# Dealing the gate products of a decoder merge out between the steps of its prompt attention

## The chip, the cores and the metric

One core of a Trainium2 chip runs the whole program in one launch; everything is float32. The metric is the device time of an execution in microseconds. The kernel before takes 2867.99 us (median of 3 runs, 2867.73 to 2868.76).

## The reference, cut to what matters

One decoder layer for two groups of tokens with the same weights: a prompt of 256 tokens and 8 sequences of 8 new tokens with a paged cache of 2048. So T = 320 token columns. The part that the change concerns:

```
u = RMSNorm(x)                                   # 2048 x 320
z = u @ W_in                                     # q, k, v, small gates, and the merge gates g_A, g_B (2 x 2048 columns)
A = FoX(u); B = NSA(u)                           # attention, 8 heads each, prompt and decode
h = x + W_out( sigmoid(g_A) * (A @ U_A) + sigmoid(g_B) * (B @ U_B) )
y = h + HierMoE(RMSNorm(h))
```

g_A and g_B depend on u alone and so may be computed at any time after the norm; A @ U_A and B @ U_B need the finished attention of prompt and decode tokens.

## The kernel before, in words

The order is written out by hand: seven stages, each a block in which every engine runs its own list, with semaphores between them, and all engines meet at the end of a block.

1. `compress_stage` (the first 278 us of the profile): compressed cache keys and values.
2. `project_stage` (to 803 us): the norm gives `ut`, u in 16 tiles of 128 x 320. Each of 44 weight tiles (1 MB, 128 x 2048, from `w_proj`) comes through the ring `wring` of 4 slots and makes 16 matmuls of 128 x 128 weights by 320 columns (L426). At its end SP stores `ut` to memory (L393) and waits for all stores.
3. `prompt_stage` (to 1076 us): first a chain of small steps for the decode tokens (compressed scores L687, their softmax, transposes L693, importance L697, block selection L701, compressed outputs L703, running sums of the forget gates L714 to L719, one round per head). Then 32 units of prompt attention, (fox, cmp, slc, win) for each of 8 heads, in a pipeline over rounds u = 0 to 33. In round u TensorE computes the scores of unit u (L733 to L743), transposes the probabilities of unit u-1 (L753, L757), and multiplies those of unit u-2 with the values (L773 to L784). VectorE does `front(u)` (mask, maximum) and then `back(u-1)` (scaling by the reciprocal sum); ScalarE does the exponential of u, the copy of the transposed probabilities of u-1 and, for fox and win, the copy of the output of u-2 from PSUM. Outputs of fox go to banks 4 and 5 in turn, those of NSA to 6 and 7.
4. `decode_stage` (to 1530 us): 172 MB of cache stream through four buffers, one of which is the memory of `ut`, another most of `wring`. SP reads the page numbers first and then issues the loads. Once the last values are used it prefetches the first four tiles of the merge (L1009).
5. `merge_stage` (to about 2080 us): `ut` is loaded again (L1275). For each of 16 column tiles j three weight tiles arrive: gate A, gate B, and the stacked U. That is 32 + 16 = 48 matmuls of 320 columns (L1301 for the gates, L1305 for the rest); ScalarE takes the sigmoid from PSUM (L1343), VectorE multiplies and adds (L1370 to L1374). Then the product with W_out (L1327, L1331), 512 columns each.
6. `route_stage` and 7. `experts_stage` (to the end): 52 tiles of expert work; each result is copied to one of NY = 10 buffers (L1953), stored by a ScalarE DMA (L1915), and the buffer is waited for before it is used again (L1952).

Of the kernel before, what the change touches and what calls it, by code (L numbers as in the profile page):

```python
# [19 lines left out]
FP32 = mybir.dt.float32  # L20
# [5 lines left out]
P = 128  # L26
DM = 2048
# [308 lines left out]
def project_stage(nc, m, a):  # L336

    with ExitStack() as ctx:
# [11 lines left out]
        x_in, csw_in, u_out = sem("x_in"), sem("csw_in"), sem("u_out")  # L350
# [13 lines left out]
        def _(sp):  # L364
# [216 lines left out]

def prompt_stage(nc, m, a):

    with ExitStack() as ctx:
        def sem(name):
            return ctx.enter_context(nc.semaphore(name))
        low, mid_ = Pieces(m.flat[:, 0:8192]), Pieces(m.utf)
# [12 lines left out]
        arow = mid_(P, P * FH)  # L600
# [15 lines left out]
        pair, sm, pt, st = mid_(P, 2, NSB * NSB), mid_(P, 2, 384), mid_(P, 2, 384), mid_(P, 2, 8)  # L616
# [20 lines left out]
        @block.sync  # L637
        def _(sp):
            sp.dma_start(cc, a["consts"][:, extra0:extra1]).then_inc(c_in, 16)
            sp.dma_start(m.blockof, a["consts"][0:NSB, extra1:extra1 + PAGES * P]).then_inc(m.rows_in, 16)  # L640
            for dst, name in ((m.row_of, "row_of"), (m.row_win, "row_win"), (m.row_new, "row_new"), (m.row_rep, "row_rep")):
                at, n = C_AT[name]
                sp.dma_start(dst, a["consts"][0:dst.shape[0], at:at + n]).then_inc(m.rows_in, 16)

# [8 lines left out]
        def _(pe):  # L653
            def done(ins):
                ins.then_inc(pe_s, 1)
# [25 lines left out]
            for g in range(G):  # L681
                last = nc.tensor.matmul(m.bank[0:NC_P, 6, g * P:(g + 1) * P], hidp[:, 1, g * NC_P:(g + 1) * NC_P],
                                        m.p("w2_v"), start=True, stop=True)
            done(last)

            for j in range(NB * G):
                last = nc.tensor.matmul(m.bank[32 * (j % 4):32 * (j % 4) + 32, 7, (j // 4) * NC_S:(j // 4 + 1) * NC_S],  # L687
                                        qs[:, j * R * NT:(j + 1) * R * NT],
                                        m.kcs[:, j, 0:NC_S], start=True, stop=True)
            done(last)  # L690
            pe.wait_ge(ds, V_PROBS)
            for t in range(4):
                last = nc.tensor.transpose(m.bank[0:NC_S, 0, t * P:(t + 1) * P], pcs[:, t, :], ident)  # L693
            done(last)
            pe.wait_ge(ds, V_PCT)
# [3 lines left out]
            done(last)  # L699
            pe.wait_ge(ds, V_SEL)  # L700
            done(nc.tensor.transpose(m.bank[0:NSB, 2, 0:P], rank, ident))  # L701
            for j in range(NB * G):
                last = nc.tensor.matmul(m.bank[:, 7, j * 32:(j + 1) * 32], m.vcs[0:NC_S, j, :],  # L703
# [5 lines left out]
            for h in range(FH):  # L709
                if h < 2:  # L710
                    pe.wait_ge(ds, V_SELT)
                else:
                    pe.wait_ge(acs, 2 + h - 1)
                done(nc.tensor.transpose(m.bank[:, 3 + h % 2, 0:P], lf_v[:, :, h], ident))  # L714
# [3 lines left out]
                nc.tensor.matmul(m.bank[:, 5 + h % 2, 0:P], m.c("tri"), lft[:, h % 2, :], start=True, stop=False)  # L718
                done(nc.tensor.matmul(m.bank[:, 5 + h % 2, 0:P], psum_pg[:, h:h + 1].broadcast_to([P, P]),  # L719
# [4 lines left out]
            for u in range(NU + 2):  # L724
                if u < NU:
# [18 lines left out]
                    last.then_inc(sc_done, 1)  # L744
                if 1 <= u <= NU:
# [13 lines left out]
                    last.then_inc(ptr_done, 1)  # L759
                if u >= 2:  # L760
# [3 lines left out]
                    if kind == "fox":  # L764
                        if h >= 2:
                            pe.wait_ge(o_kept, 2 * (h - 2) + 1)
                        ob, first, end = m.bank[:, 4 + h % 2, :], True, True
                    else:
                        if kind == "cmp" and h >= 2:
                            pe.wait_ge(o_kept, 2 * (h - 2) + 2)  # L770
                        ob, first, end = m.bank[:, 6 + h % 2, :], kind == "cmp", kind == "win"
# [16 lines left out]
        def _(act):  # L788
# [5 lines left out]
            nc.scalar.activation(pcs, pcs, ACT.Exp, scale=SCALE).then_inc(exp_done, 1)  # L794
            for h in range(FH):
                act.wait_ge(pe_s, E_PAST + 2 * h)
                if h >= 2:
                    act.wait_ge(pe_s, E_PAST + 2 * (h - 2) + 1)
                nc.scalar.activation(lft[:, h % 2, :], m.bank[:, 3 + h % 2, 0:P], ACT.Copy).then_inc(acs, 1)
            for u in range(NU + 2):  # L800
                if u < NU:
# [4 lines left out]
                    for t in range(2):  # L806
# [3 lines left out]
                        last.then_inc(exp_done, 1)  # L810
                if 1 <= u <= NU:
# [8 lines left out]
                if u >= 2:  # L820
                    v = u - 2
                    kind, h = units[v]
                    if kind in ("fox", "win"):
                        act.wait_ge(pv_done, v + 1)
                        dst = m.zt[:, FQ + h, 0:TP] if kind == "fox" else m.onsa[:, h, 0:TP]
                        nc.scalar.activation(dst, m.bank[:, (4 if kind == "fox" else 6) + h % 2, 0:TP], ACT.Copy
                                             ).then_inc(o_kept, 1)

        @block.vector
        def _(dve):  # L830
# [17 lines left out]
            step(nc.vector.tensor_copy(vcp[0:NC_P, :, :], m.bank[0:NC_P, 6, 0:G * P].rearrange("p (g d) -> p g d", g=G)))  # L848

            dve.wait_ge(pe_s, E_CMPS)  # L850
            s7 = m.bank[:, 7, 0:4 * NC_S].rearrange("p (t n) -> p t n", t=4)
# [16 lines left out]
            pa = pair[:, 0, :].rearrange("p (j i) -> p j i", i=NSB)  # L868
            pb = pair[:, 1, :].rearrange("p (j i) -> p j i", i=NSB)
            nc.vector.tensor_tensor(pa, vi, vj, ALU.is_gt)  # L870
            step(nc.vector.tensor_tensor(pb, vi, vj, ALU.is_equal))
            step(nc.vector.tensor_tensor(pair[:, 1, :], pair[:, 1, :], c("before"), ALU.mult))
            step(nc.vector.tensor_tensor(pair[:, 0, :], pair[:, 0, :], pair[:, 1, :], ALU.add))
# [13 lines left out]
            cmo = m.bank[:, 7, :].rearrange("p (b h t) -> p h b t", b=NB, t=NT)  # L887
# [3 lines left out]
            for h in range(FH):  # L891
                dve.wait_ge(pe_s, E_PAST + 2 * h + 1)
                step(nc.vector.tensor_scalar(m.ncum[:, :, :, h], m.bank[:, 5 + h % 2, 0:P].rearrange(
# [56 lines left out]
def decode_stage(nc, m, a):  # L950

    with ExitStack() as ctx:
# [15 lines left out]
        set_used, wk_in, wv_in = sem("set_used"), sem("wk_in"), sem("wv_in")  # L968
        cum_turned, cum_ready, qp_ready = sem("cum_turned"), sem("cum_ready"), sem("qp_ready")
        new_done, win_done, mx_step, nm_ready, exp_done = (  # L970
# [1188 lines left out]
```

## Time and profile before

| | us |
|---|---|
| median of 3 runs | 2867.99 |
| profiled execution | 2867.84 |
| its span, first to last instruction | 2865.2 |
| TensorE matmuls busy | 2239.0 (78%) |
| VectorE busy | 439.8 (15%) |
| ScalarE busy | 242.7 (8%) |
| prompt units (885 to 1076.4 us): TensorE busy | 120.67 of 191.40 |

A share of busy time is a mean over stages with different limits. In the projection and the merge TensorE is busy without a gap, in the decode stage and the experts the DMA engines are, and in the prompt stage neither is. The granted clock of TensorE is one of two levels, 1.0 (2.4 GHz) or 0.5 (1.2 GHz); a number between them is a mean over a stretch. The row of a float32 matmul counts two instructions for each matmul of the program.

### The profile page before, as it was taken

The numbers are of one execution on the slowest core, as the hardware profiler recorded it, in microseconds if no ns is written. First come the engines' busy times: TensorE is split into PE (matmuls) and PEld (weight loads), VectorE is DVE, ScalarE is ACT, GpSimd is POOL, SyncE is SP. The second block draws the span as 40 slices with busy tenths as digits, with TensorE's granted clock in tenths as the row PEclk, the third lists the DMA queues.
The fourth block names the chain that finished last, engine by engine and source line by source line (L and its number), as shares of the span: only waits on it lengthen the run. The fifth ranks groups of instructions, "written<-read, shape, count | busy, mean of one in ns | idle before, by whom it ended". The sixth has DMA issues, their size and how long they took to land. (4 is left out here: it accounts for less than half of the span.)

```text
span 2865.2 us, 33848 instructions
## 1 busy us (share of the span) xinstructions
PE 2239.0 (78%) x13995; PEld 1383.9 (48%) x13995; DVE 439.8 (15%) x1051; ACT 242.7 (8%) x633; POOL 68.4 (2%) x74
## 2 busy tenths in 40 slices
PE   8998499999756666787886999999974666677752
PEld 7887277777544443334444777774332222232220
DVE  0000100015713331111110000000013111111102
ACT  0000100012101220011010000000010000000000
POOL 0000000000000000000000000000001010000000
PEclk9999799999855557988998999999986787878876
DMA  5543533322220008999995333333246998888875
GB/s 184 158 136 105 180 128 117 120 100 103 101 98 0 0 0 338 413 411 409 411 405 244 130 120 117 126 123 117 103 170 266 408 372 342 366 342 366 359 311 204
DMA packets 117221, 609.24 MB, mean 213 GB/s; under 512 B 18940, under 2 KB 19213, under 8 KB 79309
## 3 DMA queue, kind: packets, MB, share of 16 engines
q1 hardware_dynamic: 100446, 556.72, 50.0%
q0 software_dynamic: 9200, 31.89, 3.0%
q10 hardware_dynamic: 7456, 18.88, 1.7%
q8 instruction: 95, 1.56, 0.2%
q14 instruction: 24, 0.20, 0.0%
HBM read 700.33 MB, written 36.98 MB: 257 GB/s over the span
## 5 line engine op out<-in xcount | busy, mean ns | idle before, releaser
L426 PE MATMUL bank<-ut,wring 128*128 128x320 f32 x1408 | 382.3, 433 | 0.0
L426 PEld LDWEIGHTS bank<-ut,wring 128*128 128x128 f32 x1408 | 267.1, 190 | 110.3 <-issue 1.1
L1301 PE MATMUL bank<-ut,wring 128*128 128x320 f32 x1024 | 280.9, 435 | 17.1 <-DMA ut<-u_kept 17.1
L1301 PEld LDWEIGHTS bank<-ut,wring 128*128 128x128 f32 x1024 | 195.9, 191 | 99.2 <-DMA ut<-u_kept 17.2
L1881 PE MATMUL bank<-wdn,par 128*32 128x512 f32 x512 | 94.4, 873 | 100.6 <-issue 99.8
L1852 PE MATMUL bank<-wgu,arena 128*32 128x512 f32 x1024 | 122.5, 618 | 12.3 <-DMA wgu<-in_w_gu 12.3
L1327 PE MATMUL bank<-wring,arena 128*128 128x512 f32 x256 | 118.4, 605 | 3.1 <-DVE arena L1374 1.6
L247 PE MATMUL bank<-arena,wring 128*128 128x256 f32 x512 | 117.4, 393 | 1.5 <-DMA arena<-in_cmp_kv 1.5
L1863 PE MATMUL bank<-stack,arena 128*128 128x32 f32 x416 | 63.2, 299 | 66.1 <-ACT arena L1905 66.1
L561 DVE RECIPROCAL snew<-snew 128x320 f32<-128x320 f32 x30 | 64.5, 2150 | 313.7 <-ACT snew L530 313.7
L247 PE MATMUL bank<-zt,wring 128*128 128x256 f32 x512 | 111.8, 379 | 0.0
L1863 PEld LDWEIGHTS bank<-stack,arena 128*128 128x128 f32 x416 | 57.2, 213 | 111.5 <-ACT arena L1905 81.4
L247 PEld LDWEIGHTS bank<-arena,wring 128*128 128x128 f32 x512 | 101.0, 198 | 16.3 <-DMA arena<-in_cmp_kv 1.6
L247 PEld LDWEIGHTS bank<-zt,wring 128*128 128x128 f32 x512 | 97.0, 190 | 13.0
L1881 PEld LDWEIGHTS bank<-wdn,par 128*32 128x32 f32 x512 | 18.6, 138 | 135.5 <-issue 133.9
L1327 PEld LDWEIGHTS bank<-wring,arena 128*128 128x128 f32 x256 | 46.0, 189 | 74.8 <-issue 70.3
L1852 PEld LDWEIGHTS bank<-wgu,arena 128*32 128x32 f32 x1024 | 35.2, 117 | 94.9 <-issue 80.5
L1032 PE MATMUL bank<-arena,wring 128*32 128x512 f32 x384 | 51.7, 677 | 34.9 <-DMA arena<-in_kv_k 29.3
L1852 PE MATMUL bank<-wgu_x,arena 128*32 128x512 f32 x640 | 78.6, 634 | 0.0
L1219 DVE TENSOR_REDUCE wring<-bank 128x1 f32<-128x512 f32 x32 | 22.1, 691 | 337.1 <-PE bank L1040 337.1
L1831 PE MATMUL bank<-cst,arena 128*128 128x128 f32 x208 | 37.3, 330 | 44.1 <-DMA arena<-u_tok,tok_at 40.7
L1305 PE MATMUL bank<-zt,wring 128*128 128x320 f32 x256 | 71.5, 432 | 0.0
(392 smaller groups left out, 2125.8 us busy)
## 6 DMA issues: line engine op xcount, KB each, us to landing
wgu<-in_w_gu SPq DMA_DIRECT2D x128, 1024.0 KB, 18.1
wring<-in_w_merge SPq DMA_DIRECT2D x64, 1024.0 KB, 4.8
wdn<-in_w_dn SPq DMA_DIRECT2D x32, 2048.0 KB, 27.9
wring<-in_w_proj SPq DMA_DIRECT2D x44, 1024.0 KB, 4.8
arena<-in_kv_k SPq DMA_DIRECT2D x64, 640.0 KB, 10.0
arena<-in_kv_v SPq DMA_DIRECT2D x64, 640.0 KB, 16.4
wring<-in_kv_k SPq DMA_DIRECT2D x32, 640.0 KB, 15.3
ut<-in_kv_k SPq DMA_DIRECT2D x32, 640.0 KB, 16.9
```

The lines of the kernel that those rows point to most:

```text
L247: last = nc.tensor.matmul(out, w1[kv][:, part * CSTR + l, :], rows[s][:, :, kv, :, l, :].rearrange("p q g j -> p g q j"), start=(l == 0), ...
L426: last = nc.tensor.matmul(m.bank[:, 2 + s % 2, 0:T], m.wring[:, s, k * P:(k + 1) * P], m.ut[:, k, :], start=(k == 0), stop=(k == KD - 1))
L561: step(nc.vector.reciprocal(rn[:, q, :], rn[:, q, :]))
L1032: nc.tensor.matmul(m.bank[rows(j), q, :], qp[:, b % 2, 96 * j + 32 * e:96 * j + 32 * e + 32], k[:, :, h * P:(h + 1) * P], start=(e == 0), ...
L1219: nc.vector.tensor_reduce(mx[:, q:q + 1], m.bank[:, q, :], AX.X, ALU.max)
L1301: last = nc.tensor.matmul(m.bank[:, bk + t, 0:T], w, m.ut[:, k, :], start=(k == 0), stop=(k == KD - 1))
L1305: last = nc.tensor.matmul(m.bank[:, bk + 2 + k // FH, 0:T], w, src, start=(k % FH == 0), stop=(k % FH == FH - 1))
L1327: nc.tensor.matmul(m.bank[:, OB[half][2 * b + c], :], mix[:, k, b * P:(b + 1) * P], m.wring[:, s, i * 1024 + c * 512:i * 1024 + (c + 1) * ...
L1831: last = nc.tensor.transpose(m.bank[:, 2 + kg % 2, j * P:(j + 1) * P], e.xg[:, k * P:(k + 1) * P], m.c("ident"))
L1852: last = nc.tensor.matmul(m.bank[q * TW:(q + 1) * TW, i % 2, :], u[:, k, lo:lo + TW], w[:, k, :], start=(k < 4), stop=(k >= KD - 4))
L1863: last = nc.tensor.matmul(m.bank[:, 4 + i % 2, f * TW:(f + 1) * TW], e.part[:, f * P:(f + 1) * P], e.stack[:, :], start=True, stop=True)
L1881: last = nc.tensor.matmul(m.bank[j * TW:(j + 1) * TW, 6 + i % 2, :], e.hid[:, i % 2, f * TW:(f + 1) * TW], w[:, f, cols:cols + 512], start ...
```

## The change

**The gate products move from the merge to the prompt stage.** The 32 gate tiles (A and B of each j in turn) become 512 matmuls, numbered 0 to 511. A function `fill(upto)` on TensorE issues them up to a given number, and it is called at fixed places of the prompt stage: 8 before the transposes of the compressed probabilities, 4 before the importance, 18 before the selection, 8 in each of the eight rounds of the running sums (94 in all), and the other 418 in three portions of 4 or 5 in each of the 34 rounds: before the scores, before the transposes and before the values. At the first matmul of a tile TensorE waits for the tile's weights and, from the third tile on, for the copy of the tile two before it out of PSUM. The products go to banks 6 and 7 in turn, so the attention's outputs keep one bank each (4 for fox, 5 for NSA), and their first matmul waits for the copy of the head before.

**Their results go to memory.** ScalarE copies each tile to one of two buffers `raw` (a function `keep`, called after the exponential of a round), and SP stores it to a tensor `gates`. SP loads the weights through three slots of `wring`; a load waits for the use of the slot, and each store stands behind a load in SP's list.

**The merge** loads `gates` four column pairs at a time into the memory of `ut`, takes the sigmoid of 640 columns from there, and has 16 matmuls for each j in place of 48. It is written out without loops.

**Around it:** the store of `ut` and its reload go. The table `blockof` is loaded at the start of the decode stage. Several pieces of the prompt stage's working memory move. To save semaphores, the window keys and values of the decode share one, so that the window scores of a sequence wait for its window values too; VectorE's chains in the decode share one; and NY is 8.

```diff
-            sp.wait_ge(z_done, NW)
-            sp.dma_start(a["u_t"], m.ut[:, :, :]).then_inc(u_out, 16)
-            sp.wait_ge(u_out, 16)
...
+EARLY = 94
+FILL = {"probs": 8, "pct": 12, "sel": 30, "past": [30 + 8 * (h + 1) for h in range(FH)],
+        "unit": [EARLY + -(-(2 * KD * KD - EARLY) * (i + 1) // (3 * (4 * H + 2))) for i in range(3 * (4 * H + 2))]}
...
+            sp.wait_ge(pe_s, E_HIDV)
+            for n in range(2 * KD):
+                if n >= 3:
+                    sp.wait_ge(g_done, n - 2)
+                sp.dma_start(m.wring[:, n % 3, :], a["w_gate"][n, :, :]).then_inc(gw_in[n % 3], 16)
+                if n >= 4:
+                    store(n - 4)
+            for n in range(2 * KD - 4, 2 * KD):
+                store(n)
+            for s in range(2):
+                sp.wait_ge(g_out[s], 16 * KD)
...
+            def fill(upto):
+
+                nonlocal given
+                while given < upto:
+                    n, k = given // KD, given % KD
+                    if k == 0:
+                        pe.wait_ge(gw_in[n % 3], 16 * (n // 3 + 1))
+                        if n >= 2:
+                            pe.wait_ge(g_kept, n - 1)
+                    last = nc.tensor.matmul(m.bank[:, 6 + n % 2, 0:T], m.wring[:, n % 3, k * P:(k + 1) * P], m.ut[:, k, :],
+                                            start=(k == 0), stop=(k == KD - 1))
+                    if k == KD - 1:
+                        last.then_inc(g_done, 1)
+                    given += 1
...
+                fill(FILL["past"][h])
...
             for u in range(NU + 2):
+                fill(FILL["unit"][3 * u])
...
+                fill(FILL["unit"][3 * u + 1])
                 if 1 <= u <= NU:
...
+                fill(FILL["unit"][3 * u + 2])
                 if u >= 2:
...
+            def keep(upto):
+
+                nonlocal kept
+                while kept < upto:
+                    act.wait_ge(g_done, kept + 1)
+                    if kept >= 2:
+                        act.wait_ge(g_out[kept % 2], 16 * (kept // 2))
+                    nc.scalar.activation(raw[:, kept % 2, :], m.bank[:, 6 + kept % 2, 0:T], ACT.Copy).then_inc(g_kept, 1)
+                    kept += 1
...
+                keep((FILL["unit"][3 * u - 1] if u else FILL["past"][FH - 1]) // KD)
                 if 1 <= u <= NU:
...
+            keep(2 * KD)
...
-                for t in range(3):
-                    s = (3 * jj + t) % SLOTS
...
+            for j in range(KD):
+                act.wait_ge(g_in[j // GJ % 2], 16 * (j // (2 * GJ) + 1))
+                if j >= 2:
+                    act.wait_ge(mix_ready, j - 1)
+                nc.scalar.activation(sg[:, j % 2, :], gates[:, j // GJ % 2, j % GJ, :], ACT.Sigmoid).then_inc(sig_ready, 1)
...
-NY = 10
+NY = 8
```

TensorE in the prompt stage before, from the first scores (a fox unit) to the scores of the third unit:

```order
L739 MATMUL bank<-zt 128x128
L742 MATMUL bank<-arena,cst 128x128
L739 MATMUL bank<-zt 128x256
L742 MATMUL bank<-arena,cst 128x256
L733 MATMUL bank<-arena,zt 128x15 x2
L757 MATMUL bank<-cst,ut 128x128 x3
L739 MATMUL bank<-zt 128x128
L739 MATMUL bank<-zt 128x256
```

The same place of the changed kernel, where L686 is `fill`:

```order
L686 MATMUL bank<-ut,wring 128x320 x5
L782 MATMUL bank<-zt 128x128
L785 MATMUL bank<-arena,cst 128x128
L782 MATMUL bank<-zt 128x256
L785 MATMUL bank<-arena,cst 128x256
L686 MATMUL bank<-ut,wring 128x320 x12
L776 MATMUL bank<-arena,zt 128x15 x2
L686 MATMUL bank<-ut,wring 128x320 x4
L801 MATMUL bank<-cst,arena 128x128 x3
L686 MATMUL bank<-ut,wring 128x320 x8
L782 MATMUL bank<-zt 128x128
L782 MATMUL bank<-zt 128x256
```

Between scores and transposes there are now four gate matmuls, between the transposes and the next scores eight, four of them before the values and four behind (in the first rounds, which have no values yet, they stand together).

ScalarE in the same rounds of the changed kernel: L865 the exponentials, L849 `keep`, L877 the copy of the transposed probabilities, L885 an output:

```order
L865 ACTIVATE arena<-arena 128x15 x2
L849 ACTIVATE selmask<-bank 128x320
L877 ACTIVATE arena<-bank 128x384
L865 ACTIVATE arena<-arena 128x128
L865 ACTIVATE arena<-arena 128x256
L849 ACTIVATE selmask<-bank 128x320
L877 ACTIVATE arena<-bank 15x256
L885 ACTIVATE zt<-bank 128x256
```

A copy of a gate tile stands behind the exponentials of the round after the one in which the tile's last matmul was issued.

TensorE in the merge before, two column tiles:

```order
L1301 MATMUL bank<-ut,wring 128x320 x32
L1305 MATMUL bank<-zt,wring 128x320 x8
L1305 MATMUL bank<-onsa,wring 128x320 x8
L1301 MATMUL bank<-ut,wring 128x320 x32
L1305 MATMUL bank<-zt,wring 128x320 x8
L1305 MATMUL bank<-onsa,wring 128x320 x8
```

And in the changed kernel, three column tiles:

```order
L1365 MATMUL bank<-zt,wring 128x320 x8
L1365 MATMUL bank<-onsa,wring 128x320 x8
L1365 MATMUL bank<-zt,wring 128x320 x8
L1365 MATMUL bank<-onsa,wring 128x320 x8
L1365 MATMUL bank<-zt,wring 128x320 x8
L1365 MATMUL bank<-onsa,wring 128x320 x8
```

Of each column tile's 48 matmuls the 32 of the gates are gone.

## Rows read from the trace of the kernel before

**Rows 1.** The page, the span in 40 slices of 71.6 us: busy tenths and granted clock.

```profile
PE   8998499999756666787886999999974666677752
PEclk9999799999855557988998999999986787878876
```

**Rows 2.** Windows: length, busy us (x instructions) of PE, PEld, DVE, ACT, POOL; clock, DMA, GB/s.

```profile
700.00:760.00 60.00, 60.00 (x234) 42.58 (x233) 42.76 (x56) 11.54 (x28) 0.00 (x0) 1.00 0.14 51
844.50:885.00 40.50, 24.84 (x123) 20.38 (x123) 17.15 (x39) 4.14 (x11) 0.00 (x0) 0.54 0.00 0
885.00:1076.40 191.40, 120.67 (x377) 81.91 (x376) 63.40 (x265) 49.95 (x176) 0.00 (x0) 0.52 0.00 0
...
1101.50:1124.00 22.50, 17.10 (x272) 6.29 (x268) 4.01 (x10) 0.38 (x1) 0.00 (x0) 1.00 1.02 413
...
1546.00:1551.00 5.00, 4.95 (x9) 3.19 (x10) 0.00 (x0) 0.00 (x0) 0.00 (x0) 0.50 0.92 394
1553.00:1966.00 413.00, 411.38 (x1526) 289.64 (x1525) 22.09 (x48) 13.98 (x32) 0.00 (x0) 1.00 0.34 122
```

**Rows 3.** Timeline of one round in the prompt units: start, duration, [idle before].

```profile
980.77 0.56 DVE L905 TENSOR_TENSOR ut<-bank,arena 128x384 f32<-128x384 f32 x1 [5.89 <-PE bank L742]
...
983.01 0.19 ACT L807 ACTIVATION_READ_ACCUMULATOR ut<-ut 128x1 f32 x1
983.08 0.90 PE L757 MATMUL bank<-cst,ut 128*128 128x128 f32 x3 [2.35 <-DVE ut L935]
```

**Rows 4.** Timeline of the merge's start and two later column tiles.

```profile
1527.13 2.09 SPq L1009 DMA_DIRECT2D wring<-in_w_merge  x4
...
1546.05 20.01 PE L1301 MATMUL bank<-ut,wring 128*128 128x320 f32 x64 [17.09 <-DMA ut<-u_kept]
...
1574.51 17.39 PE L1301 MATMUL bank<-ut,wring 128*128 128x320 f32 x64
...
1600.35 17.39 PE L1301 MATMUL bank<-ut,wring 128*128 128x320 f32 x64
```

**Rows 5.** DMAs: KB each, median us to landing; last, those of tile y_slot.

```profile
wring<-in_w_merge SPq DMA_DIRECT2D x64, 1024.0 KB, 4.8
arena<-in_cmp_kv SPq DMA_DIRECT2D x64, 256.0 KB, 3.0
wring<-in_win_v SPq DMA_DIRECT2D x8, 512.0 KB, 18.0
```

```profile
DMA to landing us min/median/max: 5.8/9.4/10.1
```

**Rows 6.** Waits of SP's queue, 786 to 804 us: total, times, longest.

```profile
SPq L395 <- DMA out_k_nsa<-zt: 6.5, 1, 6.5
SPq L338 <- DMA u_kept<-ut: 6.0, 1, 6.0
```

**Rows 7.** Timeline of the prompt stage's first part, TensorE.

```profile
851.85 1.22 PE L693 MATMUL bank<-cst,arena 128*127 128x128 f32 x4 [4.00 <-DVE arena L857]
...
854.52 1.91 PE L697 MATMUL bank<-arena 127*128 127x33 f32 x8 [1.45 <-DVE arena L861]
...
863.65 0.42 PE L701 MATMUL bank<-cst,arena 128*33 128x128 f32 x1 [7.22 <-DVE arena L875]
...
863.87 6.88 PE L703 MATMUL bank<-arena 127*128 127x32 f32 x32
...
870.55 0.45 PE L714 MATMUL bank<-cst,ut 128*128 128x128 f32 x1
...
872.39 0.42 PE L714 MATMUL bank<-cst,ut 128*128 128x128 f32 x1
```

**Rows 8.** The copies of 320 columns by line L503: min/median/max ns.

```profile
L503 ACT ACTIVATE zt<-bank x30: 437/437/437, 355.8 to 605.5; 128x320 f32 x28, 128x320 f32<-128x320 f32 x2
```

**Rows 9.** Timeline of one decode sequence: issue of window values, window scores.

```profile
1153.16 1.29 SPq L998 DMA_DIRECT2D wring<-in_win_v  x1
...
1173.98 1.06 PE L1068 MATMUL bank<-arena,wring 128*32 128x512 f32 x8
```

More of the change, by code:

```diff
@@ L615, in prompt_stage @@
         selt = piece(P)
-        pair, sm, pt, st = mid_(P, 2, NSB * NSB), mid_(P, 2, 384), mid_(P, 2, 384), mid_(P, 2, 8)
+        pair = [low(P, NSB * NSB), spare(P, NSB * NSB)]
+        sm, pt, st = low(P, 2, 384), low(P, 2, 384), low(P, 2, 8)
+        raw = spare(P, 2, T)
+        gw_in, g_out = [sem(f"gw_in{s}") for s in range(3)], [sem(f"g_out{s}") for s in range(2)]
+        g_done, g_kept = sem("g_done"), sem("g_kept")
         idx = ctx.enter_context(nc.sbuf_tensor("idx", [P, 1], I32))
@@ L681, in _ @@
             for g in range(G):
-                last = nc.tensor.matmul(m.bank[0:NC_P, 6, g * P:(g + 1) * P], hidp[:, 1, g * NC_P:(g + 1) * NC_P],
+                last = nc.tensor.matmul(m.bank[0:NC_P, 0, g * P:(g + 1) * P], hidp[:, 1, g * NC_P:(g + 1) * NC_P],
                                         m.p("w2_v"), start=True, stop=True)
@@ L686, in _ @@
             for j in range(NB * G):
-                last = nc.tensor.matmul(m.bank[32 * (j % 4):32 * (j % 4) + 32, 7, (j // 4) * NC_S:(j // 4 + 1) * NC_S],
+                last = nc.tensor.matmul(m.bank[32 * (j % 4):32 * (j % 4) + 32, 3, (j // 4) * NC_S:(j // 4 + 1) * NC_S],
                                         qs[:, j * R * NT:(j + 1) * R * NT],
@@ L690, in _ @@
             done(last)
+            fill(FILL["probs"])
             pe.wait_ge(ds, V_PROBS)
@@ L694, in _ @@
             done(last)
+            fill(FILL["pct"])
             pe.wait_ge(ds, V_PCT)
@@ L699, in _ @@
             done(last)
+            fill(FILL["sel"])
             pe.wait_ge(ds, V_SEL)
@@ L702, in _ @@
             for j in range(NB * G):
-                last = nc.tensor.matmul(m.bank[:, 7, j * 32:(j + 1) * 32], m.vcs[0:NC_S, j, :],
+                last = nc.tensor.matmul(m.bank[:, 3, j * 32:(j + 1) * 32], m.vcs[0:NC_S, j, :],
                                         pct[0:NC_S, j * 32:(j + 1) * 32], start=True, stop=True)
@@ L764, in _ @@
                     if kind == "fox":
-                        if h >= 2:
-                            pe.wait_ge(o_kept, 2 * (h - 2) + 1)
-                        ob, first, end = m.bank[:, 4 + h % 2, :], True, True
-                    else:
-                        if kind == "cmp" and h >= 2:
-                            pe.wait_ge(o_kept, 2 * (h - 2) + 2)
-                        ob, first, end = m.bank[:, 6 + h % 2, :], kind == "cmp", kind == "win"
+                        if h >= 1:
+                            pe.wait_ge(o_kept, 2 * (h - 1) + 1)
+                        ob, first, end = m.bank[:, 4, :], True, True
+                    else:
+                        if kind == "cmp" and h >= 1:
+                            pe.wait_ge(o_kept, 2 * (h - 1) + 2)
+                        ob, first, end = m.bank[:, 5, :], kind == "cmp", kind == "win"
                     if kind == "cmp":
@@ L794, in _ @@
             nc.scalar.activation(pcs, pcs, ACT.Exp, scale=SCALE).then_inc(exp_done, 1)
+            kept = 0
+            def keep(upto):
[6 more added lines that the diff above has]
+                    kept += 1
             for h in range(FH):
+                keep((FILL["past"][h - 1] if h else FILL["sel"]) // KD)
                 act.wait_ge(pe_s, E_PAST + 2 * h)
@@ L1174, in _ @@
         def _(dve):
-            sums, outs, maxes = Chain(dve, sum_step), Chain(dve, out_step), Chain(dve, mx_step)
+            step = Chain(dve, dve_step)
             def queries(b):
@@ L1266, in merge_stage @@
         ss_ready, tok_in = sem("ss_ready"), sem("tok_in")
-        u_in = sem("u_in")
-        NW = 4 * KD
+        g_in = [sem(f"g_in{s}") for s in range(2)]
+        NW = 2 * KD
         base = list(m.w_uses)
@@ L1337, in _ @@
         def _(act):
-            def gates(j, jj):
-                for t in range(2):
-                    act.wait_ge(tile_done, j * 3 + t + 1)
-                    if t == 0 and not (isinstance(j, int) and j < 2):
-                        act.wait_ge(mix_ready, j - 1)
-                    nc.scalar.activation(sg[:, jj % 2, t, :], m.bank[:, 4 * (jj % 2) + t, 0:T], ACT.Sigmoid
-                                         ).then_inc(sig_ready, 1)
-            for j in range(4):
-                gates(j, j)
-            with act.Fori(1, KD // 4) as i:
-                for jj in range(4):
-                    gates(i * 4 + jj, jj)
+            for j in range(KD):
+                act.wait_ge(g_in[j // GJ % 2], 16 * (j // (2 * GJ) + 1))
+                if j >= 2:
+                    act.wait_ge(mix_ready, j - 1)
+                nc.scalar.activation(sg[:, j % 2, :], gates[:, j // GJ % 2, j % GJ, :], ACT.Sigmoid).then_inc(sig_ready, 1)
             for half in range(2):
```

163 lines of the change are left out of this document (78 added, 85 removed).

## The prediction

> **What bounds the kernel now.** I read the slices first. The reader is to see that TensorE is nearly always busy and mostly at its high clock, and that in slices 12 to 15 both fall together: about six tenths busy and a clock of 0.5 [rows 1]. That is the prompt stage. The windows say it exactly: in the 34 rounds of the units TensorE works 120.67 of 191.40 us, at a mean clock of 0.52, with no DMA at all, while the merge is a solid block at 1.00 (411.38 of 413.00 us) with the DMA engines at 0.34 [rows 2]. Then I read one round of the timeline: the scores end at 980.74, VectorE masks them at 980.77, and TensorE starts the transposes of the round before only at 983.08, after 2.35 us of idleness, because its list puts scores, transposes and values in one order and VectorE does `front(u)` before `back(u-1)` [rows 3]. TensorE and VectorE take turns; neither bounds the stage, their sum does. Last, the merge: 48 matmuls take 1600.35 - 1574.51 = 25.84 us, or 0.538 us each at full clock, and TensorE stood 17.09 us before its first one, for the reload of `ut` [rows 4].
>
> So the change takes work from a place where every microsecond of it is paid and puts it where TensorE idles 70.7 us (191.4 - 120.7). It can't be hidden there: 418 x 0.538 = 225 us of work go into 70.7 us of gaps. What decides is the rest of the bill, above all the clock.
>
> **The clock.** In the rounds before, matmuls run at 1.2 GHz, since the short bursts never keep the engine busy. The projection's last part has nearly the mixture that the changed rounds will have: 16 matmuls of 320 columns, then a few small ones, without gaps, and it is granted 1.00 (its window from 700 us) [rows 2]. Even a stretch with waits, 17.10 us busy of 22.50 in the decode stage, is at 1.00 (the window from 1101.5 us) [rows 2]. I take the changed rounds to run at 2.4 GHz; TensorE's own work in them, 120.67 us at 0.52, then takes 120.67 x 0.52 = 63 us. This is the main gain that the diff doesn't show, and the main risk. From idle to the high clock costs about 5 us at 0.50, as at the merge's start (the window from 1546 us) [rows 2].
>
> A rule speaks against it: the Trainium skill, page "TensorE: Matmul & The Clock Gate", section "A second HAM failure mode: psum-queue depth-cycling", tells of a kernel whose brief idle moments between groups of matmuls made the clock swing between its levels. By it the dealt-out rounds, with a wait in each, would pay part of the stage at 1.2 GHz, the third rival below; the 1.00 of the decode stretch above, at three quarters busy, speaks against it.
>
> **Part by part**, against the profiled execution's own 2867.84 us (0.15 us from the median; so its sum is taken as it stands).
>
> 1. *Merge, gates gone:* 512 x 0.538 = -275.6 us [rows 4]. TensorE bounds there before and after: a column tile falls from 25.84 to 8.6 us, its one weight tile lands in 4.8 [rows 5], and VectorE's and ScalarE's part is under 2 us (22.09 and 13.98 us busy in 413 [rows 2]). The loads of `gates` (1.3 MB each, at the 394 GB/s of the merge's start [rows 2] some 3.3 us) are needed only when the third column tile begins, 17 us in.
> 2. *Merge, start:* the first weight tile is issued at 1527.13 and lands 4.8 us later, near 1531.9; TensorE started at 1546.05 because of `ut` [rows 4, 5]. -14.1 us. The bounds are -12, if four tiles issued together delay each other, and -15.7, if TensorE could start as the block does, at 1530.33.
> 3. *End of the projection:* SP waits 6.5 us for the store of k and then 6.0 more for that of `ut` [rows 6]. The second goes, -6.0; at most -12.5, if the first went too.
> 4. *First part of the prompt stage*, 94 gate matmuls, 50.6 us. TensorE had waits of 4.00, 1.45 and 7.22 us there [rows 7]. The 8 before the first begin when the weights land, some 1.7 us late, and at low clock (up to 1.076 each): they run 3.7 us past the wait. The 4 take 2.2 for 1.45 (+0.7), the 18 take 9.7 for 7.22 (+2.5). TensorE's own steps get faster with the clock, L703 from 6.88 to about 3.5 and L693, L697 from 3.1 to about 1.6: -5. The eight rounds of the running sums took 1.84 each (872.39 - 870.55); they now take 4.3 of gate work, which covers the copy that was waited for, plus about 0.7: 8 x 5.0 - 8 x 1.84 = +25.3, with small waits say +26. Sum +28. Bounds: +10 (94 matmuls less all idle and half of TensorE's busy 24.84 in this window), and +87 with all at 1.2 GHz, 94 x 1.076 = 101 less 14 covered.
> 5. *The 34 rounds:* own work 63 us, gate work 418 x 0.538 = 225. The portion between scores and transposes, 4 x 0.538 = 2.15, doesn't quite fill the 2.35 us of VectorE and the 0.2 us by which matmuls are issued before they end: 0.4 us in each of the 24 fox, slc and win rounds, +10. Then a wait that is new. A gate tile is copied out of PSUM behind the exponentials of a round. By the table of numbers, of the 26 tiles begun in the rounds 8 begin in the portion between scores and transposes (tiles 7, 10, 14, 17, 20, 24, 27, 30); for all but tile 10 the tile two before was finished only in the round before this one, so its copy stands behind this very round's exponentials. These end 983.20 - 980.74 = 2.46 us after the scores [rows 3], the copy takes 0.44 [rows 8]: 2.9 us, of which the 0 to 3 matmuls ahead of the boundary cover up to 1.6. Summed over the seven about 15 us; some 4 of them lie where TensorE would have waited for VectorE anyway: +11. Together 63 + 225 + 10 + 11 = 309 for 191.4: +117.6. Bounds: +96 if the gaps and the new wait cost nothing (288 us), and +384 at 1.2 GHz (2 x 63 + 418 x 1.076 = 576).
> 6. *End of the prompt stage:* the last tile is copied after the last output (0.44), stored (164 KB; 256 KB land in 3.0 us [rows 5]), and SP waits for it: +3.7. Bounds 3 and 6.
> 7. *At nothing, or nearly:* `blockof` moves ahead of SP's page reads, +0.4 us of issue, while TensorE idles until the first keys land. The window scores now wait for the window values too: issued at 1153.16, they land 18.0 us later [rows 5], at about 1171.2, and TensorE reaches the scores at 1173.98 [rows 9], so 2.8 us of cover; without it 8 x 1.3 us (512 KB at 400 GB/s) = 10. NY = 8: a result is stored within 10.1 us [rows 5], and eight tiles take over 80 us. One bank for each output: the copy of the head before is two rounds old. SP's list: a weight load stands behind a store whose data is one tile old, and has two tiles (17 us) for its 4.8. The copies put 0.44 us each into ScalarE, busy 49.95 of 191.4 [rows 2].
>
> Sum: -275.6 - 14.1 - 6.0 + 28 + 117.6 + 3.7 + 0.4 = -146. **2867.8 - 146 = 2722 us.**
>
> **Rivals.**
> - *Everything is covered* (chance 0.14). The idle terms of part 5 vanish because VectorE's work slides under other portions: 21 us less, 2701. For it: three portions per round and 8 free rounds of cmp. Against: the list is strict, and the boundary waits follow from it.
> - *The forecast as summed* (0.65): 2706 to 2745.
> - *The clock swings* (0.15). The boundary waits of about 3 us, or the small matmuls of L744 and the running sums, let it fall for a part of the stage. All of it at 1.2 GHz costs 384 - 117.6 + 87 - 28 = 325 us more; a fifth of it 65: 2787, and the case spans 2745 to 2840. For it: the rounds before are at 0.5 though 63% busy. Against: the stretches at 1.00 named above.
> - *The clock stays low throughout* (0.05). The stage's matmuls never leave 1.2 GHz; then the moved 512 matmuls cost 551 us where the merge paid 276, and the total is -146 + 325 = +179: 3047 us, slower. It turns from a gain to a loss when 146/325 = 45% of the stage is at the low clock. For it: 128-column and 15-column steps stand between the portions. Against: gate work would be three quarters of the time.
> - *It doesn't do what it says* (0.01): TensorE's list shows the 512 matmuls moved, so only a memory wait could spoil it, for instance weights that land late; each tile has 10 us or more, against 4.8.
>
> **How the numbers follow.** The forecast is the likeliest case, 2722. The range leaves out less than 0.2: from 2692 (everything covered, and the projection's end and the merge's start at their better bounds) to 2785 (a fifth of the stage at the low clock). A measurement of this kernel can tell 0.2% from no change, about 6 us; all cases but the last two lie over 25 us below. Slower takes the low clock and the worst of the swings, 0.06; the band around no change 0.01; faster 0.93.
>
> **What would show it.** In the profile after: the windows of the rounds at a clock over 0.95 and TensorE over 93% busy, their length near 309 us, and the running sums' rounds near 5.0 us. Among the waits TensorE <- ScalarE's copy in the filling line, seven or so in the rounds, up to 2.9 us, about 15 us in all. The merge's products without gates near 140 us, starting within 3 us of the block. No TensorE wait for gate weights beyond the first. Wrong would be: a clock near 0.5 to 0.8 in the rounds (then third or fourth rival), a wait of TensorE on a DMA in every tile, a decode stage longer than 454 us by more than 3, or experts that changed.

## The result, and the profile after

The changed kernel takes **2725.4 us** (median of 4 runs, 2723.7 to 2729.0) where the kernel before takes 2868.4 in the same comparison (4 runs, 2867.7 to 2868.9): ratio 0.9505, 95% interval 0.9492 to 0.9519. The forecast was 2722 us, in the likeliest case's own 2706 to 2745. The profiled execution took 2729.0 us, 2727.1 of them span; it is the slowest of the four, so the ledger below sums to -138 where the medians differ by 143.

The page's slices of the span, now 68.2 us each (busy tenths of TensorE, then its granted clock):

```profile
PE   8999299999949999985878788999936566676761
PEclk8999699998967999997899888999967878787876
```

Slices 14 to 17, which lie in the prompt stage, are now 9 and 9; before, slices 13 to 15 stood at 6 and 5 [rows 1]. The windows say what is behind it; the columns are those of [rows 2].

```profile
844.50:911.40 66.90, 63.45 (x273) 46.96 (x273) 15.45 (x36) 5.04 (x14) 0.00 (x0) 0.95 0.33 118
911.45:1224.74 313.29, 294.57 (x1212) 204.90 (x1212) 63.30 (x264) 58.05 (x201) 0.00 (x0) 0.99 0.29 95
1684.90:1691.00 6.10, 6.02 (x12) 3.98 (x13) 0.00 (x0) 0.00 (x0) 0.00 (x0) 0.53 1.01 426
1691.00:1827.00 136.00, 134.86 (x502) 94.89 (x500) 21.70 (x48) 11.68 (x16) 0.00 (x0) 1.00 0.48 177
```

The second row is the 34 rounds: TensorE works 294.57 of 313.29 us at a clock of 0.99, where it worked 120.67 of 191.40 at 0.52 [rows 2]. The counts tell that the work was added: 1212 instructions for 377, and 836 of the difference are 418 gate matmuls of two instructions each. 418 x 0.538 = 225 us of the 294.6 are theirs, so the rounds' own work fell from 120.7 to 69.6 us: the same instructions at the high clock (not all of the 69.6 is work, as the fourth experiment shows). The last two rows are the merge, now 142 us for 418.

TensorE's waits in the rounds (what was waited for, total us, times, longest):

```profile
PE bank L686 <- ACT selmask L849: 15.0, 7, 2.9
PE bank L797 <- DVE arena L995: 2.7, 4, 0.7
PE bank L801 <- DVE arena L995: 0.8, 4, 0.2
```

The first is the wait that the change brought: a gate tile may not begin before the tile two before it is copied out of its bank, and that copy stands in ScalarE's list behind the exponentials. One of the seven, on the timeline (start, duration, [idle before and its releaser]):

```profile
1199.26 0.82 PE L782 MATMUL bank<-zt 128*128 128x128 f32 x4
1200.11 0.56 DVE L965 TENSOR_TENSOR arena<-bank,arena 128x384 f32<-128x384 f32 x1 [6.12 <-PE bank L782]
...
1202.36 0.19 ACT L865 ACTIVATION_READ_ACCUMULATOR arena<-arena 128x1 f32 x1
1202.45 0.41 ACT L849 ACTIVATE selmask<-bank 128x320 f32<-128x320 f32 x1
...
1203.01 3.86 PE L686 MATMUL bank<-ut,wring 128*128 128x320 f32 x8 [2.93 <-ACT selmask L849]
```

The scores end at 1200.08, VectorE masks them, ScalarE takes the exponentials until 1202.55, and only then copies a tile that was finished a round before. TensorE stands for 2.93 us behind a copy of 0.41 us that had nothing to wait for.

The merge's start, and the product behind the merge:

```profile
1680.12 2.02 SPq L1070 DMA_DIRECT2D wring<-in_w_merge  x4
...
1684.98 6.30 PE L1365 MATMUL bank<-zt,wring 128*128 128x320 f32 x12 [3.04 <-DMA wring<-in_w_merge]
...
1827.46 2.84 PE L1380 MATMUL bank<-wring,arena 128*128 128x512 f32 x6 [1.60 <-DVE arena L1417]
```

TensorE starts 4.86 us after the first weight load is issued, on that load, instead of 18.92 us, on `ut` [rows 4].

The whole difference, from the two profiled executions (us, before and after):

```
stretch                                          before    after   change  forecast
start to the prompt stage's first load           803.29   799.86    -3.4    -6.0
first part of the prompt stage                    82.46   111.59   +29.1   +28
34 rounds                                        190.07   313.29  +123.2  +117.6
end of the rounds to the first cache load          9.80    12.99    +3.2    +4.1
decode, to the first w_merge load                441.51   442.39    +0.9     0
to the merge's first product                      18.92     4.86   -14.1   -14.1
merge                                            417.84   142.48  -275.4  -275.6
rest                                             901.31   899.64    -1.7     0
sum                                             2865.20  2727.10  -138.1  -146
```

The first line holds two things. From the issue of the store of k to the stage's first load it is 8.85 us for 14.90 before, -6.05; but the projection reached that store 2.6 us later (791.01 for 788.39). Over all ten profiles the store is issued between 785.3 and 791.0, with the projection's code up to it unchanged, so this part is a spread between executions.

### The profile page after: what moved, and what is told of

The parts are those of the page before. It is cut to its first block and busy times, and to the rows that moved or that the text cites. A ratio compares the mean times of both kernels' runs of the same rounds, so it can differ in the third digit from the quotient of the medians.

```text
span 2727.1 us, 33661 instructions
## 1 busy us (share of the span) xinstructions
PE 2180.7 (80%) x13995; PEld 1346.6 (49%) x13995; DVE 440.5 (16%) x1051; ACT 251.4 (9%) x649; POOL 68.3 (3%) x74
## 5 line engine op out<-in xcount | busy, mean ns | idle before, releaser
L423 PE MATMUL bank<-ut,wring 128*128 128x320 f32 x1408 | 382.6, 433 | 0.0
L686 PE MATMUL bank<-ut,wring 128*128 128x320 f32 x1024 | 301.6, 441 | 18.1 <-ACT selmask L849 15.0
L686 PEld LDWEIGHTS bank<-ut,wring 128*128 128x128 f32 x1024 | 190.6, 193 | 94.2 <-issue 26.8
L1380 PEld LDWEIGHTS bank<-wring,arena 128*128 128x128 f32 x256 | 46.0, 189 | 74.7 <-issue 70.2
L1279 DVE TENSOR_REDUCE wring<-bank 128x1 f32<-128x512 f32 x32 | 22.1, 692 | 332.1 <-PE bank L1101 332.1
```

The costliest lines, as they stand in the source:

```text
L423: last = nc.tensor.matmul(m.bank[:, 2 + s % 2, 0:T], m.wring[:, s, k * P:(k + 1) * P], m.ut[:, k, :], start=(k == 0), stop=(k == KD - 1))
L686: last = nc.tensor.matmul(m.bank[:, 6 + n % 2, 0:T], m.wring[:, n % 3, k * P:(k + 1) * P], m.ut[:, k, :], start=(k == 0), stop=(k == KD - 1))
L1380: nc.tensor.matmul(m.bank[:, OB[half][2 * b + c], :], mix[:, k, b * P:(b + 1) * P], m.wring[:, s, i * 1024 + c * 512:i * 1024 + (c + 1) * ...
```

## The experiments

Theory A is the prediction's account of the stage: the gate work fills the gaps that TensorE and VectorE make in turn, most of all the one between scores and transposes; its load holds the clock high and so halves the rounds' own work; what is left over is the waits for copies and some of VectorE's. Its rival is put, with its numbers, in each expectation, which was on record before its kernel ran. In each run the verdict is read from the length of the rounds and from TensorE's waits in them. The first four experiments form one series, in which the kernel before took 2865.5 us, the last four a second one, in which it took 2862.5; total times are compared inside a series.

**The copy ahead of the exponentials.** In ScalarE's list of a round the copy moves from behind the exponentials to the start of the round. Its argument changes with it: it now also takes a tile that ends in the first portion of the same round. Nothing else changes.

```diff
             for u in range(NU + 2):
+                keep(FILL["unit"][3 * u] // KD)
                 if u < NU:
                     kind, h = units[u]
...
-                keep((FILL["unit"][3 * u - 1] if u else FILL["past"][FH - 1]) // KD)
```

> The changed kernel with one thing moved: ScalarE copies a finished gate tile out of PSUM ahead of a round's exponentials, not behind them. Theory A (the waits of TensorE for that copy, 15.0 us in 7 waits, are on the path, and nothing else takes their place): they vanish, the rounds fall from 313 to about 300 us, total 2711 to 2715. Theory B (TensorE would have waited for VectorE in those rounds anyway, so the wait only changes its name): 2721 to 2726, and TensorE's waits for VectorE grow by what the others lose.

Measured: 2709.6 us (2706.6 to 2713.3), ratio 0.9459 (0.9446 to 0.9471). The rounds take 298.55 us, 14.7 less, and no wait for the copy is left. VectorE's waits grew a little, from 3.5 to 6.1 us. The rounds, and what TensorE waits for in them:

```profile
907.69:1206.24 298.55, 292.36 (x1212) 203.98 (x1212) 63.19 (x264) 60.17 (x201) 0.00 (x0) 1.00 0.30 100
```

```profile
PE bank L797 <- DVE arena L995: 4.7, 7, 0.7
PE bank L801 <- DVE arena L995: 1.4, 7, 0.2
```

So the seven waits cost 12.4 us net of 15.0, and some 2 us more went with the clock that fell at the last of them (below); here it stays at 1.00. Theory A holds: the rounds were to fall to about 300 us, and the total is 1.4 us under its range. All further kernels contain this edit.

**All gate work in one lump ahead of the rounds.** The table lets all 418 matmuls run before the first scores, and the rounds run bare.

```diff
-        "unit": [EARLY + -(-(2 * KD * KD - EARLY) * (i + 1) // (3 * (4 * H + 2))) for i in range(3 * (4 * H + 2))]}
+        "unit": [2 * KD * KD] * (3 * (4 * H + 2))}
```

> As e1, but all 418 gate matmuls of the rounds stand in one block ahead of the first round, none between the steps. Theory A (the dealing out gains in two ways, by filling the 70.7 us of idleness and by keeping the clock high): the block takes 225 us at clock 1.00, the rounds behind it are again about 190 us at a clock near 0.52, total about 2827. Theory B (the rounds got shorter by themselves, through the other memory and the single output banks, or a warm engine stays warm): rounds clearly under 190 us, or at a clock over 0.8, total under 2790.

Measured: 2819.9 us (2817.9 to 2821.6), ratio 0.9845 (0.983 to 0.986). The lump and the bare rounds, as windows:

```profile
905.00:1128.16 223.16, 223.16 (x830) 157.54 (x829) 0.00 (x0) 10.95 (x25) 0.00 (x0) 1.00 0.41 133
1128.16:1315.30 187.14, 116.97 (x377) 79.83 (x375) 63.16 (x264) 49.98 (x176) 0.00 (x0) 0.55 0.00 1
```

The same 1207 to 1212 instructions take 410.3 us this way and 298.6 dealt out: 112 us for the order alone. 64 us of that are idleness: 70.2 us in the bare rounds (187.14 - 116.97) for 6.1 dealt out. The other 48 are the clock: TensorE is busy for 340.1 us in all, and for 292.4 dealt out. The bare rounds fall to 0.55 although they begin right behind 223 us at 1.00, and their 117 us of work take about 67 when dealt out. Theory A holds (it had 190 us for the rounds and 2827 in all); theory B is excluded, since the rounds, with the other memory and the single output banks, are only 3 us shorter than the 190.07 before.

**Half the work before the scores, half before the values, none between scores and transposes.** This keeps TensorE loaded in each round, but leaves the pause open in which it waits for VectorE.

```diff
-        "unit": [EARLY + -(-(2 * KD * KD - EARLY) * (i + 1) // (3 * (4 * H + 2))) for i in range(3 * (4 * H + 2))]}
+        "unit": [EARLY + -(-(2 * KD * KD - EARLY) * n // (2 * (4 * H + 2)))
+                 for u in range(4 * H + 2) for n in (2 * u + 1, 2 * u + 1, 2 * u + 2)]}
```

> As e1, but each round's gate matmuls stand half before the scores and half before the values, none between scores and transposes, so that nothing lies beside VectorE's part. Theory A (only the portion between scores and transposes hides anything, and the clock stays high by the others alone): clock over 0.95, TensorE idle 70 to 80 us waiting for VectorE, rounds 365 to 375 us, total 2775 to 2787. Theory B (a pause of 2.4 us in each round lets the clock fall, as in the kernel before): clock near 0.5 to 0.7, rounds over 450 us, total over 2870. Theory C (the clock is what the dealing out brings, the filled pauses are worth little): rounds under 330 us, total under 2745.

Measured: 2791.6 us (2790.5 to 2792.6), ratio 0.9745 (0.9731 to 0.976). The rounds, then its waits:

```profile
905.18:1287.40 382.22, 313.52 (x1212) 217.47 (x1212) 63.15 (x264) 60.85 (x201) 0.00 (x0) 0.94 0.24 78
```

```profile
PE bank L802 <- DVE arena L996: 46.1, 23, 2.4
PE bank L798 <- DVE arena L996: 22.6, 8, 2.8
```

All 31 pauses are there, 68.7 us, and TensorE's clock still is 0.94. This run parts the two gains: with the load but without the right place, the pauses stay (68.7 us) and the clock is mostly won (313.5 us busy, for 223.2 + 117.0 = 340.1 in the lump). So A holds in its mechanism, and its numbers come out short: it wanted a clock over 0.95, 365 to 375 us for the rounds and at most 2787 in all. B and C are far off. Here the clock does fall at some pauses: by the trace's clock records twelve times in the rounds, each time in or right behind a pause of 2.3 to 2.8 us, of which there are 23, and never at one of the eight of 1.36 us; a gate instruction's mean is 461 ns, where it is 435 in the first experiment. One such place:

```profile
1115.04 0.39 PE L798 MATMUL bank<-cst,arena 128*15 128x128 f32 x2 [2.82 <-DVE arena L996]
1115.27 5.08 PE L687 MATMUL bank<-ut,wring 128*128 128x320 f32 x12
```

Twelve instructions take 5.08 us, where twelve take 3.2 at 0.269 each: from that, some seven of them ran at 1.2 GHz.

**All work between scores and transposes.** One portion of 12 or 13 matmuls a round, in the place of the pause.

```diff
-        "unit": [EARLY + -(-(2 * KD * KD - EARLY) * (i + 1) // (3 * (4 * H + 2))) for i in range(3 * (4 * H + 2))]}
+        "unit": [EARLY + -(-(2 * KD * KD - EARLY) * n // (4 * H + 2)) for u in range(4 * H + 2) for n in (u, u + 1, u + 1)]}
```

> As e1, but all of a round's 12 or 13 gate matmuls stand between scores and transposes. Theory A (what counts is that VectorE's 2.35 us are covered; where the rest stands is all one): as e1, 2709 to 2715. Theory B (three portions are needed, since TensorE also waits for ScalarE's copies of the probabilities or outputs, or the small matmuls in a row let the clock fall): new TensorE waits on ScalarE, total over 2722.

Measured: **2697.4 us** (2696.5 to 2701.3), ratio 0.9418 (0.9405 to 0.9431), the fastest version of all, so both theories were wrong on this one.

```profile
910.88:1198.99 288.11, 288.11 (x1212) 206.60 (x1212) 63.20 (x264) 58.27 (x201) 0.00 (x0) 1.00 0.31 103
```

TensorE is never idle in the 34 rounds. Neither theory had it faster than the first experiment's kernel, which it is, by 12 us: the 6.1 us of VectorE's waits are gone, and 288.1 - 225 = 63.1 us is what the rounds' own work takes, 4.3 less than in the first experiment (292.4 - 225 = 67.4), though it is the same instructions at the same clock.

These 4.3 us are mostly waits as well, and not a price of the borders between gate and attention work. The first experiment's trace tells the two apart, by the starts of instructions at the end of a gate portion:

```profile
1007.31 2.32 PE L686 MATMUL bank<-ut,wring 128*128 128x320 f32 x8
1009.82 0.55 PE L801 MATMUL bank<-cst,arena 128*128 128x128 f32 x3 [0.20 <-DVE arena L995]
...
1020.12 2.32 PE L686 MATMUL bank<-ut,wring 128*128 128x320 f32 x8
1022.28 0.39 PE L828 MATMUL bank<-arena,vt 128*128 128x128 f32 x2
```

In the second pair the values start 2.16 us after the portion, which is 8 x 0.27: this border costs nothing, nor does any before scores (before the values of cmp it is 0.09 us, in eight rounds). In the first pair the transposes start 2.51 us after it, 0.36 late, of which the profile shows 0.20 as idle. It counts a gate instruction busy for 0.43 us, 0.16 more than its pitch, so the first 0.16 us of a wait stands in busy time. That happens before 21 of the 32 transposes of the first experiment, 3.4 us in all, and before none here, where a gate instruction is followed by the next start in 0.269 us at each of the 32. So of the 10.4 us between the two versions 9.5 are TensorE's wait for VectorE: a middle portion of 4 or 5 matmuls is a little shorter than VectorE's part, one of 12 or 13 is not. Theory A was right that VectorE's part has to be covered, but took it to be covered in the first experiment already.

**The same kernel in a second series**, beside which the three that follow ran.

> The kernel of e4 again, unchanged, as the reference for the three runs beside it on the same chip: 2694 to 2702 us by either theory; how far it comes from its first 2697 us says how small a difference between two kernels can be read.

Measured: 2699.5 us (2698.3 to 2701.5), ratio 0.943 (0.9417 to 0.9443), 2.1 us from the first series.

**Without the early 94.** From the version above; no gate work in the first part of the stage, all 512 in the rounds.

```diff
-EARLY = 94
-FILL = {"probs": 8, "pct": 12, "sel": 30, "past": [30 + 8 * (h + 1) for h in range(FH)],
+EARLY = 0
+FILL = {"probs": 0, "pct": 0, "sel": 0, "past": [0] * FH,
```

> As e4 (all of a round's gate matmuls between scores and transposes), but none of the 94 gate matmuls in the first part of the prompt stage: all 512 go into the 34 rounds, 15 or 16 in each. Theory A (in the first part about 21 us of the 94 are hidden, by its waits and by the higher clock): that part falls back from 111 to about 82 us at a clock near 0.54, the rounds grow by 94 x 0.538 = 50.6 to about 339 us, total 2715 to 2722. Theory B (the early ones hide nothing, since they run at low clock and put off the chain of steps): total 2694 to 2702, as e4.

Measured: 2726.2 us (2723.6 to 2728.6), ratio 0.9527 (0.9514 to 0.954), 26.7 us over the same-series run of the version above. The first part is 83.0 us for 112.0, the rounds 342.6 for 288.1. So the 94 cost 28.9 us in the first part and would cost 54.5 in the rounds: 50.6 for the matmuls and the rest because the rounds now begin at the low clock, which lasts from 879.96 to 888 (0.50 in that window, 1.00 in the rest of the rounds):

```profile
879.96 0.80 PE L782 MATMUL bank<-zt 128*128 128x128 f32 x2 [0.55 <-DVE ncum L953]
...
883.71 11.07 PE L686 MATMUL bank<-ut,wring 128*128 128x320 f32 x32
```

32 instructions of 0.269 would be 8.6 us. A's direction and mechanism hold; its upper bound was 4 us too low, for the cold start that it left out.

**The waits for `ut` put back.** From the version above; `ut` is stored at the end of the projection and waited for there, and TensorE waits for both loads of `gates` at the merge (the tensor's declaration and a later count of stores are left out).

```diff
-            sp.wait_ge(m.stores, 6 * 16)
+            sp.wait_ge(z_done, NW)
+            sp.dma_start(a["u_t"], m.ut[:, :, :]).then_inc(m.stores, 16)
+            sp.wait_ge(m.stores, 7 * 16)
...
+            for s in range(2):
+                pe.wait_ge(g_in[s], 16)
```

> As e4, with the two memory transfers of the kernel before put back in kind: u is stored at the end of the projection and waited for, and TensorE waits at the merge's start for both loads of gates (2.6 MB, as much as the reload of u). Nothing reads the stored u. Theory A (these two waits are paid whole): +6.0 at the projection's end and +10 to +14 at the merge's start, total 2713 to 2718, TensorE idle about 15 us before its first product of the merge. Theory B (the projection's end is set by the stores before it, and the merge makes up for a later start, because its weights come later too): total under 2706.

Measured: 2719.4 us (2718.7 to 2722.4), ratio 0.9504 (0.9491 to 0.9517), 19.9 over the same-series run. Store of k to the stage's first load: 785.62 to 800.49, 14.87 us for 8.82. And the merge's start:

```profile
1676.42 7.23 PE L1369 MATMUL bank<-zt,wring 128*128 128x320 f32 x16 [17.50 <-DMA ut<-gates]
```

17.5 us of idleness for 3.01. 6.05 + 14.49 = 20.5 us, and 19.9 were measured: both terms are on the path in full. That is theory A, with the merge's start 0.5 us over its 14 and the total 1.4 us over its range.

**The window keys on a semaphore of their own.** From the version above; the window scores wait for the keys alone, the values are waited for where they are used.

```diff
-                    "o p n -> (o p) n")).then_inc(win_in, 16)
+                    "o p n -> (o p) n")).then_inc(m.small_in, 16)
...
-                pe.wait_ge(win_in, 32 * (b + 1))
+                pe.wait_ge(m.small_in, 48 + 16 * (b + 1))
...
+                pe.wait_ge(win_in, 16 * (b + 1))
```

> As e4, but the decode's window keys and values have a semaphore each again, so that the window scores wait for their keys alone. Theory A (the values land before TensorE comes to the scores, so the shared semaphore costs nothing): within 3 us of e4, the decode stage 441 to 443 us from its first cache load to the first load for the merge. Theory B (the shared one holds TensorE back in some sequences, which the decode's first-measured 0.9 us more hints at): 3 to 10 us faster than e4.

Measured: 2698.4 us (2697.6 to 2700.6), ratio 0.9428 (0.9415 to 0.9441), 1.1 under the same-series run, within the spread. From the first cache load to the first `w_merge` load it is 442.6 us, and 442.5 in the same-series run, as theory A had it. No cost of the wait for the values can be seen.

## Why the prediction was right

Its mechanism and its sign were right, and each term stands in the profile or in a run.

- *The clock* held at 0.99 as forecast over 0.95. That the dealt-in gate work is what does it is shown by three runs: bare rounds 0.55, rounds with load and open pauses 0.94, rounds without pauses 1.00. The Trainium skill ("TensorE: Matmul & The Clock Gate", section "A second HAM failure mode: psum-queue depth-cycling") tells of a kernel whose short idle moments between groups of matmuls made the clock swing. The third experiment agrees in kind, with its twelve falls, and is mild in degree: 31 pauses of 2.0 and 2.8 us on the mean (46.1/23 and 22.6/8) leave a clock of 0.94. The prediction's reason for the low clock before, that short bursts never keep the engine busy, is too simple: the last section has a stretch that is busy throughout and at 0.50.
- *Merge, gates gone*: -275.4 for -275.6. *Merge, start*: -14.1 for -14.1. *Store of `ut`*: -6.05 for -6.0; putting the last two back cost 19.9.
- *First part*: +29.1 for +28. The running sums' rounds have a period of 4.86 us (two of their starts: 876.70 and 881.56) where I had put 5.0. One part was wrong and evened out: I let the first block of gate work run cold, and it did not.

```profile
846.05 4.57 PE L686 MATMUL bank<-ut,wring 128*128 128x320 f32 x16 [2.50 <-DMA wring<-in_w_gate]
...
868.81 0.45 PE L755 MATMUL bank<-cst,snew 128*128 128x128 f32 x1 [1.40 <-DVE onsa L949]
869.05 7.36 PE L686 MATMUL bank<-ut,wring 128*128 128x320 f32 x16
```

16 instructions in 4.57 us are at 2.4 GHz (4.3 would be full pitch); the same 16 take 7.36 at 869.05, behind the 32 small matmuls and a wait of 1.40, where I had not put a cold spell. That wait is new and was not in the sum: the first transposes of the running sums now wait until VectorE has taken the compressed outputs (`V_CMPO` in place of `V_SELT`).

- *The new wait*: 7 waits, 15.0 us, longest 2.9, as worked out from the table of numbers; that the copy's place in ScalarE's list causes them is shown by the first experiment.
- *Mis-sized terms of the rounds*, +123.2 for +117.6: the 63 us of own work are right, 63.1 in the fourth experiment. The 69.6 here hold some 2.5 us of waits for VectorE and 1.1 of waits for the copy that the profile counts as busy, and about 2 us of a cold spell, which the sum had at nothing. With these parts the waits are 6.0 us for VectorE and 16.1 for the copy, 22.1 together for the 21 of the sum (10 and 15, less the 4 that it let fall together); once the copy waits are gone, VectorE's are 9.5, near the 10. Another 1.3 us of the miss come from taking 191.4 us for the rounds before, which are 190.07 from their first instruction to their last. Under 1 us of the 69.6 has no cause found. The third rival, the swinging clock, is real in this small part; the first, everything covered, is what one portion per round reaches: 288.1 us in the rounds is its bound of 288.
- *At nothing*: the window wait is shown to be free. `blockof` and the last store make +3.2 together for the forecast +4.1. The change from ten to eight buffers of the experts (`NY`) and the second output bank were not undone by a run; they rest on the profile alone. The decode's +0.9 and the rest's -1.7 are left without a cause; they are of the size by which two series of one kernel differ (2.1 us).

What stays open: why the clock fell at one wait of 2.93 us and not at the other, and what makes the projection end up to 5.7 us earlier or later from one execution to the next.

## What to carry to other kernels

A stage in which TensorE and VectorE take turns can pay twice, as here: for the pauses and for its own matmuls at the low clock. Independent matmuls dealt into it returned both (225 us of gate work for 98 us of extra time in the best form), while the same work in one lump beside it returned next to nothing (410 us for 190 + 225). Put it where the pause is, in a portion longer than the pause: with 2.2 to 2.7 us of work there the rounds took 10 us more than with 6.5 to 7, nearly all of it the rest of that wait. And a copy that frees a bank for such filling work belongs ahead of whatever its engine has to wait for.

## What the hardware showed that was not expected

A pause did not by itself bring the clock down. Six of the seven waits of the rounds, two of them 2.40 and 2.93 us, were followed by a clock of 1.00 in the next 5 us, the seventh, again of 2.93 us, by 0.79 in the next 7 us. The windows behind the two of 2.93 us:

```profile
1081.00:1088.00 7.00, 6.72 (x30) 4.99 (x31) 0.11 (x1) 0.89 (x3) 0.00 (x0) 1.00 0.19 77
...
1203.00:1210.00 7.00, 6.99 (x22) 4.49 (x22) 0.52 (x2) 0.82 (x2) 0.00 (x0) 0.79 0.13 47
```

Nor did being busy bring it up: in the first part of the stage, in both kernels, TensorE works nearly without a pause on matmuls of 30 columns and stays at 1.2 GHz, here in the kernel before:

```profile
816.00:844.00 28.00, 27.95 (x132) 27.53 (x132) 0.62 (x2) 0.29 (x1) 0.00 (x0) 0.50 0.00 1
```

27.95 of 28.00 us busy, weight loads under way in 27.53 of them, and 0.50 throughout. In the changed kernel the first block of 320 columns after such a stretch ran at 2.4 GHz at once (846.05 above), but it did not raise the clock: the clock had risen in the pause before it, with no matmul running. In the kernel before it rose in the same way, in the pause from 848.00 to 851.40, and was back at 0.50 for the matmuls from 851.85 on. The changed kernel just before the block, and in its pause:

```profile
841.40:843.60 2.20, 2.15 (x35) 1.50 (x29) 1.19 (x2) 0.11 (x1) 0.00 (x0) 0.50 0.86 339
843.60:846.05 2.45, 0.00 (x0) 0.00 (x0) 1.54 (x3) 0.63 (x1) 0.00 (x0) 0.88 1.01 418
```

And SP needs 10.0 us from the start of the decode stage (its load from `consts` at 1227.73) to the first cache load (1237.73), in which its list holds only the reads of 16 page numbers; before, it was 9.80 us from the end of the rounds to the first cache load, so the time was there too.
